# An encoder layer's expert stage: TensorE's loop over experts begins at block 4, with another order of the weight ring's homes

## Chip, cores, metric

One core of a Trainium2 chip runs the whole kernel. The metric is the device time of one execution in microseconds (us); lower is better.

## What is computed

The layer has three parts, in float32: a mixer with its projections, a cross attention, and a hierarchical mixture of experts with a final RMS norm. The change touches only the third part, which is this, for 256 tokens of width 2048 and 32 experts of which each token takes two:

```python
p_group = softmax(x @ w_rg)                       # 4 groups, one is taken
fine    = (x @ w_re)[that group]                  # 8 experts in it, the two best
gate    = p_group_best * softmax(top2)
for e in range(32):                               # each token goes to two of these
    y[tok] += gate * ((silu(x[tok] @ w1[e]) * (x[tok] @ w3[e])) @ w2[e])
h = h + y
out = rms_norm(h, norm_final)
```

`w1` and `w3` are 2048 x 512 per expert and `w2` is 512 x 2048: 4,096 KB each, 12,288 KB per expert, all of which are read whatever the tokens chose.

## The kernel before

**Blocks.** The expert stage is a row of blocks, one per expert, with 32 places for tokens; an expert with more tokens than that gets overflow blocks at the end, whose table `over_blocks` (VectorE, L2663) and `over_table` (L2689) work out, with one small product on TensorE between them (L1295). TensorE's part of block `n` is `block_n` (L1288): first the rest of the block before (`products`: `sums` at L1231, `rank_rows` at L1199, four `down` steps with W2 at L1247), then `gather` of the next block's tokens (L1187), then four `up` steps with W1 and four with W3 (L1219). Between the W3 steps stand the four `comb` steps of the block before (L1267), each of which waits for VectorE's `add` (L2588) of the step ahead. `down` of a block waits for VectorE's `gating` (L2570, semaphore `e_h`), `comb` for `picked` and `down_lo`. VectorE's program is written in the same order: gating, pick, `down_lo`, tokens, four adds, then the next block.

**The weight ring.** SyncE issues every load, in the order W1(0), W3(0), W2(0), W1(1), W3(1), W2(1), ... The q-th of these 4,096 KB matrices is called load q here, so that q = 3n - 1 is W2(n-1), 3n is W1(n) and 3n + 1 is W3(n). There are five homes of 32 KB per partition, numbered 0 to 4; `double_slots` (L173) says which home each load goes to. Before load q SyncE waits until TensorE has used the load that lay in that home last, and everything behind it in SyncE's program waits too. A load is one DMA of 4,096 KB (L632), save that home 1 is in two places and takes two of 2,048 KB (L573), and that the first and last loads are split (L573, L578, L626, L627).

Before, loads 0 to 16 go round the homes 0 1 2 3 4. From load 17 = 3 x 6 - 1 on, six loads make a turn over homes 2 3 4 0 1 4, so that in two blocks the ring returns to its start: W3 always lies in home 4 and waits for the W3 three loads back; all others wait for the load six back. The last loads, from 89, take the home that was used longest ago.

**Loops.** TensorE's program is written out for blocks 0 to 5; blocks 6 to 29 are a hardware loop of 12 passes of two blocks, and blocks 30 and 31 are written out again. ScalarE has the same start (`LOOP_AT`), VectorE's loop starts at block 7 whatever `LOOP_AT` is.

**Norm weights.** The 2048 weights of the final norm (`fgain`) are spread over all partitions by TensorE, 16 x 64 columns at a time, with 32 products of a 32 x 64 tile per half (L1284 and the weight loads that go with it), into PSUM banks 6 and 7; ScalarE copies the 1024 columns of each half out (L1791). One half goes ahead of block 3, the other ahead of block 4; each waits until the adds of the block before have ended, because `comb` uses the same banks. The small product of the overflow table stands ahead of block 5 (`OV_AT`), and `over_blocks` stands behind block 2's part in VectorE's program.

Of the kernel before, what the change touches and what calls it, by code (L numbers as in the profile page):

```python
# [16 lines left out]
ACT = mybir.ActivationFunctionType  # L17
# [7 lines left out]
P = 128  # L25
# [10 lines left out]
NE = 32  # L36
NG = 4
PG = NE // NG
ECH = 4
# [5 lines left out]
OVG = 8  # L45
ROWS = D // GW
NO_ROW = 2 * T * ROWS * ROWS
OV_AT = 5
LOOP_AT, LOOP_N = 6, 24
GAIN_AT = (3, 4)  # L50
GAIN_ROWS = 32
assert OVB % OVG == 0
EPS = 1e-6
# [119 lines left out]
def double_slots(order):  # L173

    first, last = 3 * LOOP_AT - 1, 3 * (LOOP_AT + LOOP_N) - 1
    homes = [q % 5 for q in range(first)]
    turn = [(first + r) % 5 for r in range(5)]
    turn.append(turn[2])
    homes += [turn[r % 6] for r in range(last - first)]
    while len(homes) < len(order) // 2:  # L180
        homes.append(min(range(5), key=lambda d: max(q for q, at in enumerate(homes) if at == d)))
    return homes


# [50 lines left out]
def flat(v):  # L235
    if len(v.shape) == 3:
        return v.rearrange("p a b -> p (a b)")
    return v.rearrange("p a b c -> p (a b c)")
# [12 lines left out]
def program(nc, ins, out, dbg=None):  # L251
    dbg = dbg or {}
    with ExitStack() as ctx:
# [16 lines left out]
        gate_sel, ident = front[:, 108 + KT:124 + KT], front[:, 124 + KT:124 + KT + P]  # L270
# [4 lines left out]
        ps = ctx.enter_context(nc.psum_tensor("ps", [P, 8, 512], F32))  # L275
# [84 lines left out]
        fgain, sq_out = arena(56, D), extra(0, 1024)  # L360
        gain_cut = D // GAIN_ROWS
# [44 lines left out]
        order = load_order()  # L406
# [52 lines left out]
        S = {}  # L459
# [200 lines left out]
        @block.gpsimd  # L660
        def _(pool):
            nc.gpsimd.memset(one_pp, 1.0).then_inc(S["pool_step"], 1)
            nc.gpsimd.memset(gone, 1.0).then_inc(S["pool_step"], 1)
            nc.gpsimd.memset(buf["mv"][:, :, :, P:P + 1], 1.0).then_inc(S["pool_step"], 1)
            for s in range(2 * HG_LEVELS):
                w, half = s // HG_LEVELS, 1 << (s % HG_LEVELS)
                u = 0 if w == 0 else 1
                cut = lambda x: flat(x).rearrange("p (b u t) -> p b u t", u=2, t=half)[:, :, u, :]
                pool.wait_ge(S["h_exp"], s + 1)
                if s >= 1:  # L670
                    pool.wait_ge(S["h_pe"], s)
                nc.gpsimd.tensor_tensor(cut(hqk[s % 2]), cut(he[s % 2]), cut(buf["hff" if w == 0 else "hfb"]),
                                        ALU.mult).then_inc(S["h_mulk"], 1)


            def gained(m):

                for q in (0, 2):
                    j = DONE[q][1]
                    pool.wait_ge(S["c_add"], m * 4 + (q + 1))  # L680
                    nc.gpsimd.tensor_tensor(hg[:, j, 0:1024], h[:, j, 0:1024], fgain[:, 0:1024], ALU.mult).then_inc(S["f_gain"], 1)

            pool.wait_ge(S["gain_act"], len(GAIN_AT))
            pool.wait_ge(S["tab_dve"], 1)
            nov = pool.value_load(table[0:1, 96:97], min_val=0, max_val=OVB)
            pool.wait_ge(S["up_used1"], (NE - 1) * ECH)
            nc.gpsimd.tensor_copy(z_fold, bc_mid(stack, P // EB)).then_inc(S["z_pool"], 1)
            for b in range(ROWS):
                own = slice(EB * b, EB * (b + 1))
                pool.wait_ge(S["z_pool"], 1 + b)  # L690
                nc.gpsimd.tensor_copy(z_gain[own, :], fgain[own, GW * b:GW * (b + 1)]).then_inc(S["z_pool"], 1)
            pool.wait_ge(*z_is("gain"))
            gained(NE - 2)
            pool.wait_ge(S["out_done"], 16 * NT)
            pool.wait_ge(*z_is("out"))
            nc.gpsimd.indirect_dma_start(out[0].rearrange("t (b n) -> (t b) n", n=GW), bass.IndirectOffsetOnAxis(z_row, 0), z_out, None,
                                         bounds_check=T * ROWS - 1, oob_is_err=False).then_inc(S["rows_done"], 16)
            with pool.Fori(0, OVB // OVG) as a:
                with pool.If(a * OVG < nov):
                    with pool.Fori(0, OVG) as c:  # L700
                        gained(a * OVG + c + NE - 1)
# [5 lines left out]
        def _(pe):  # L707
# [543 lines left out]
            def comb(of, q, b0=6, behind=0, at=None):  # L1251

                n = of.done
                u, j = (q // 2, q % 2) if at is None else at
                if q == 0:
                    pe.wait_ge(S["pick_all"], n + 1)
                    pe.wait_ge(S["ev_lo"], n + 1)
                if of.turn is None and of.like + 1 in GAIN_AT and q == 0:
                    pe.wait_ge(S["gain_act"], GAIN_AT.index(of.like + 1) + 1)
                if of.turn is None and of.like == OV_AT - 1 and q == 0:  # L1260
                    pe.wait_ge(S["tab_dve"], 1)
                if not (isinstance(n, int) and 4 * n + q <= behind):
                    pe.wait_ge(S["c_add"], n * 4 + (q - behind))
                for part in (d_hi, d_lo):
                    for b in range(2):
                        rows_ = slice(EB * (2 * u + b), EB * (2 * u + b + 1))
                        last = mm(ps[:, b0 + b, :], pick[rows_, j * P:(j + 1) * P], part[rows_, :],  # L1267
                                  start=(part is d_hi), stop=(part is d_lo))
                last.then_inc(S["c_pe"], 1)
# [5 lines left out]
                for i in range(ECH):  # L1275
                    down(at, i)

            def spread_gain(part, back):

                pe.wait_ge(S["fgain_in"], 16)  # L1280
                pe.wait_ge(S["c_add"], 4 * back.n)
                for r in range(GAIN_ROWS // 2):
                    k, c0 = part * GAIN_ROWS // 2 + r, r * gain_cut
                    last = mm(ps[:, 6 + c0 // 512, c0 % 512:c0 % 512 + gain_cut], ident[0:GAIN_ROWS, k:k + 1].to_broadcast([GAIN_ROWS, P]), gain_rows,  # L1284
                              start=True, stop=True)
                last.then_inc(S["gain_pe"], 1)

            def block_n(at, back, par, then=True, counts=False):  # L1288

                if at.like in GAIN_AT and at.turn is None:  # L1290
                    spread_gain(GAIN_AT.index(at.like), back)
                if counts:
                    pe.wait_ge(S["r_dve"], 4)
                    pe.wait_ge(S["c_add"], 4 * back.n)
                    mm(ps[:, 7, 0:2 * OVB], ones, flat(ov_rhs), start=True, stop=True).then_inc(S["r_pe"], 1)  # L1295
                if back is not None:
                    products(back)
                    if then:
                        gather(at.n + 1)
                for i in range(ECH):  # L1300
                    up(at, 0, i, par)
                if back is None and then:
                    gather(at.n + 1)
                for i in range(ECH):
                    up(at, 1, i, par)
                    if back is not None:
                        comb(back, i)
# [39 lines left out]
            block_n(Block(0), None, 0)  # L1347
            for n in range(1, LOOP_AT):
                block_n(Block(n), Block(n - 1), n % 2, counts=(n == OV_AT))
            with pe.Fori(0, LOOP_N // 2) as a:  # L1350
                n = a * 2 + LOOP_AT
                before_n, even, odd = Block(n - 1, LOOP_AT - 1, a), Block(n, LOOP_AT, a), Block(n + 1, LOOP_AT + 1, a)
                block_n(even, before_n, 0)
                block_n(odd, even, 1)
# [20 lines left out]
        def _(act):  # L1375
# [412 lines left out]
            def spread_gain(part):  # L1788

                act.wait_ge(S["gain_pe"], part + 1)  # L1790
                fn(fgain[:, 1024 * part:1024 * (part + 1)], flat(ps[:, 6:8, :]), ACT.Copy).then_inc(S["gain_act"], 1)  # L1791

            def block_n(n, back):
                if isinstance(n, int) and n in GAIN_AT:
                    spread_gain(GAIN_AT.index(n))
                if back is not None:
                    silu(back)
                if back is not None:
                    down_out(back, back)
                up_out(n, 0)  # L1800
                up_out(n, 1)
# [64 lines left out]
            first_block(0)  # L1866
            for n in range(1, LOOP_AT):
                block_n(n, n - 1)
            with act.Fori(LOOP_AT, NE - 1) as e:
                block_n(e, e - 1)  # L1870
            act.wait_ge(S["tab_dve"], 1)
# [16 lines left out]
        def _(dve):  # L1888
# [819 lines left out]
            for j in range(NT):  # L2708
                last = V.tensor_copy(z_what[:, j, 0:1], weight[:, NE - 1, j:j + 1])
            last.then_inc(S["z_dve"], 1)  # L2710
            dve.wait_ge(S["gain_act"], len(GAIN_AT))
            nov = dve.value_load(table[0:1, 96:97], min_val=0, max_val=OVB)
            finish_n(NE - 2, NE - 2, NE - 2, 0, 0)
            rows_of_last()
# [39 lines left out]
```

## Time and profile before

| | us |
|---|---|
| median of 3 runs | 1781.37 |
| lowest, highest | 1779.4, 1783.01 |
| the profiled execution | 1779.85 |
| its span | 1777.8 |
| TensorE matmuls busy | 1559.8 (88%) |
| VectorE, ScalarE, GpSimd busy | 814.6, 506.4, 45.5 |
| moved by DMA | 559.82 MB, mean 315 GB/s |

The profile is of one execution. The span runs from its first instruction to its last; 2.05 us of the execution's time lie around it. The expert stage begins near 871 us and takes the rest. Granted clock is the share of TensorE's full clock (2.4 GHz) that it was given: 1.0 or 0.5 at any moment, something between in a mean.

### The profile page before, as it was taken

What the parts mean: (1) busy time and instruction counts of PE and PEld (TensorE: products, weight loads), DVE (VectorE), ACT (ScalarE), POOL (GpSimd) and SP (SyncE); (2) the same over time, 40 slices, a digit from 0 to 9 for tenths busy, and PEclk for the clock granted to TensorE, in tenths of its full rate; (3) what the DMA queues carried; (4) which work ended last, traced back from release to release, by engine and by line L of the source; (5) the groups of instructions that cost most, each with busy time, mean ns of one, the idle gap of its engine ahead of it and who ended that gap; (6) DMA issues with size and microseconds to landing.
All of it is one profiled execution on the core that took longest, in us unless ns stands there. A gap on an engine that the chain in (4) does not pass through costs nothing.

```text
span 1777.8 us, 24664 instructions
## 1 busy us (share of the span) xinstructions
PE 1559.8 (88%) x10444; PEld 965.0 (54%) x10444; DVE 814.6 (46%) x1171; ACT 506.4 (28%) x729; POOL 45.5 (3%) x31
## 2 busy tenths in 40 slices
PE   9999999999999999999899768787687777687776
PEld 8888888788877898888544222222122222122222
DVE  5666566799666554354434322223232323232223
ACT  6464354644455354343410000000000000000003
POOL 0000000033000000000000000000000000000001
PEclk9999999999999999999988877787877788877788
DMA  9755555454455556565799999999999999999998
GB/s 359 256 187 198 166 163 169 157 163 144 160 172 189 201 181 225 199 272 201 305 433 426 434 428 433 427 435 432 429 429 432 435 426 434 432 432 431 431 428 345
DMA packets 125418, 559.82 MB, mean 315 GB/s; under 512 B 8828, under 2 KB 66428, under 8 KB 107296
## 3 DMA queue, kind: packets, MB, share of 16 engines
q1 hardware_dynamic: 124112, 556.52, 78.7%
q10 hardware_dynamic: 1152, 2.10, 0.4%
q8 instruction: 55, 0.90, 0.2%
q14 instruction: 19, 0.16, 0.0%
q0 software_dynamic: 80, 0.15, 0.0%
HBM read 556.50 MB, written 2.36 MB: 314 GB/s over the span
## 4 chain that ended last, share of the span: by engine, by line
PE 63%; DMA 31%; DVE 4%; issue 1%; ACT 0%; SPq 0%; POOL 0%; DVEq 0%; ACTq 0%; POOLq 0%
DMA arena<-in_moe_w_dram 31%; PE ps L774 11%; PE ps L1219 9%; PE ps L809 6%; PE ps L811 6%; PE ps L810 6%; PE ps L775 6%; PE ps L1267 5%; DVE arena L2588 2%; PE ps L1247 1%; PE ps L803 1%; PE ps L804 1%; PE ps L805 1%; PE ps L1063 1%; PE ps L1044 1%; PE ps L1284 1%
## 5 line engine op out<-in xcount | busy, mean ns | idle before, releaser
L1219 PE MATMUL ps<-arena 128*32 128x512 f32 x1808 | 290.0, 752 | 168.0 <-DMA arena<-in_moe_w_dram 166.5
L1948 DVE TENSOR_TENSOR w_lo<-arena,w_hi 128x1024 fp32r<-128x1024 f32 x264 | 316.5, 1240 | 205.2 <-ACT w_hi L1436 204.2
L2588 DVE SCALAR_TENSOR_TENSOR arena<-ps,arena 128x1024 f32<-128x1024 f32 x124 | 159.2, 1284 | 427.9 <-PE ps L1267 427.9
L1436 ACT ACTIVATE w_hi<-arena 128x1024 fp32r<-128x1024 f32 x262 | 262.7, 1052 | 263.7 <-PE ps L811 125.7
L1219 PEld LDWEIGHTS ps<-arena 128*32 128x32 f32 x1808 | 51.1, 121 | 311.5 <-DMA arena<-in_moe_w_dram 167.4
L1774 ACT ACTIVATE arena<-ps 128x512 f32<-128x512 f32 x64 | 38.2, 597 | 580.8 <-PE ps L1219 580.8
L774 PE MATMUL ps<-x_both,w_hi 128*128 128x512 f32 x420 | 148.6, 398 | 0.0
L1247 PE MATMUL ps<-arena 128*32 128x512 f32 x992 | 132.3, 679 | 6.7 <-DMA arena<-in_moe_w_dram 6.1
L1267 PEld LDWEIGHTS ps<-d_hi,pick 32*128 32x128 f32 x248 | 28.9, 230 | 182.3 <-DVE arena L2588 136.5
L775 PE MATMUL ps<-x_both,w_lo 128*128 128x256 f32 x420 | 118.0, 281 | 0.0
L1267 PE MATMUL ps<-d_hi,pick 32*128 32x512 f32 x248 | 79.1, 635 | 19.7 <-DVE arena L2588 19.3
L774 PEld LDWEIGHTS ps<-x_both,w_hi 128*128 128x128 f32 x420 | 78.9, 188 | 19.3 <-issue 1.4
L774 PE MATMUL ps<-m_both,w_hi 128*128 128x512 f32 x240 | 86.4, 403 | 0.0
L2582 DVE TENSOR_TENSOR d_lo<-ps,d_hi 128x512 fp32r<-128x512 f32 x31 | 21.5, 692 | 135.5 <-ACT d_hi L1786 135.5
L775 PEld LDWEIGHTS ps<-x_both,w_lo 128*128 128x128 f32 x420 | 79.5, 189 | 0.3
L1247 PEld LDWEIGHTS ps<-arena 128*32 128x32 f32 x992 | 32.6, 124 | 85.0 <-issue 75.6
L775 PE MATMUL ps<-m_both,w_lo 128*128 128x256 f32 x240 | 67.4, 281 | 0.0
L1786 ACT ACTIVATE d_hi<-ps 128x512 fp32r<-128x512 f32 x31 | 18.5, 597 | 169.9 <-PE ps L1247 169.9
L809 PE MATMUL ps<-w_hi,x_both 128*128 128x512 f32 x160 | 63.3, 396 | 0.0
L774 PE MATMUL ps<-q_both,w_hi 128*128 128x512 f32 x180 | 63.3, 396 | 0.0
L1267 PE MATMUL ps<-d_lo,pick 32*128 32x512 f32 x248 | 62.5, 502 | 0.0
L811 PE MATMUL ps<-w_hi,x_both 128*128 128x512 f32 x160 | 62.4, 390 | 0.0
(403 smaller groups left out, 2425.8 us busy)
## 6 DMA issues: line engine op xcount, KB each, us to landing
arena<-in_moe_w_dram SPq DMA_DIRECT2D x68, 4096.0 KB, 28.5
arena<-in_moe_w_dram SPq DMA_DIRECT2D x32, 2048.0 KB, 36.3
arena<-in_w_in_dram SPq DMA_DIRECT2D x51, 1024.0 KB, 5.0
extra<-in_moe_w_dram SPq DMA_DIRECT2D x17, 2048.0 KB, 32.5
arena<-in_xa_wk_dram SPq DMA_DIRECT2D x16, 1024.0 KB, 5.2
arena<-in_xa_wv_dram SPq DMA_DIRECT2D x16, 1024.0 KB, 5.0
arena<-in_w_out_dram SPq DMA_DIRECT2D x16, 1024.0 KB, 5.1
arena<-in_xa_wq_dram SPq DMA_DIRECT2D x16, 1024.0 KB, 5.3
```

Of the source, the lines that this page charges most:

```text
L774: mm(*whole_, start=(k == 0), stop=False, skip_group_check=True)
L775: last = mm(*part_, start=False, stop=False, skip_group_check=True)
L809: mm(o_, a_hi[:, k, rows_], hi, start=(k == 0), stop=False)
L810: mm(o_, a_hi[:, k, rows_], lo, start=False, stop=False)
L811: last = mm(o_, a_lo[:, k, rows_], hi, start=False, stop=(k == KT - 1))
L1219: last = mm(ps[EB * c:EB * (c + 1), m, :], xe[par][:, ECH * i + c, :], piece(at.like, m, i)[:, c, :], start=(i == 0), stop=(i == ECH - 1))
L1247: last = mm(ps[EB * b:EB * (b + 1), 4, :], hT[:, i, :], piece(at.like, 2, i)[:, b * 512:(b + 1) * 512], start=(i == 0), stop=(i == ECH - 1))
L1267: last = mm(ps[:, b0 + b, :], pick[rows_, j * P:(j + 1) * P], part[rows_, :], start=(part is d_hi), stop=(part is d_lo))
L1436: fn(hi_ring[(2 * n + u) % 4][:], ring_a[i][:, 2 * u:2 * u + 2, :], ACT.Copy).then_inc(S["w_hi"], 1)
L1774: fn(up_ev[:, m, :].rearrange("p (c q) -> p c q", c=ECH), ps[:, m, :].rearrange("p (q c) -> p c q", c=ECH), ACT.Copy).then_inc(S["ev_g" if ...
L1948: V.tensor_tensor(w_lo[i][:, 2 * u:2 * u + 2, :], ring_a[i][:, 2 * u:2 * u + 2, :], hi_ring[(2 * n + u) % 4][:].bitcast(F32), ALU.subtract ...
L2588: V.scalar_tensor_tensor(hv, flat(ps[:, b0:b0 + 2, :]), weight_of(e, j), hv, ALU.mult, ALU.add).then_inc(S["c_add"], 1)
```

## The change

TensorE's and ScalarE's loops begin at block 4, not 6 (13 passes of two blocks on TensorE). With that the six-load turn begins at load 3 x 4 - 1 = 11 and goes over homes 1 2 3 4 0 3; home 3 now has the short wait of three loads. The last seven loads get their homes by a written list. The overflow table is made two blocks sooner: `over_blocks` behind block 0's part on VectorE, `over_table` behind block 1's, the small product ahead of block 3. Both halves of the norm weights are spread between block 3 and the loop, the second into banks 2 and 3, and TensorE waits there for both of ScalarE's copies. GpSimd's copies for the last rows wait for W2 of block 30 instead of W3, because their place is now freed by it.

```diff
-OV_AT = 5
-LOOP_AT, LOOP_N = 6, 24
-GAIN_AT = (3, 4)
+OV_AT = 3
+LOOP_AT, LOOP_N = 4, 26
+GAIN_PARTS = 2
...
-    while len(homes) < len(order) // 2:
-        homes.append(min(range(5), key=lambda d: max(q for q, at in enumerate(homes) if at == d)))
+    homes += [turn[r] for r in (0, 1, 3, 4, 2, 3, 1)]
+    assert len(homes) == len(order) // 2
...
-            pool.wait_ge(S["up_used1"], (NE - 1) * ECH)
+            pool.wait_ge(S["dn_used"], (NE - 1) * ECH)
...
-                if of.turn is None and of.like + 1 in GAIN_AT and q == 0:
-                    pe.wait_ge(S["gain_act"], GAIN_AT.index(of.like + 1) + 1)
...
-            def spread_gain(part, back):
+            def spread_gain(back):
 
                 pe.wait_ge(S["fgain_in"], 16)
-                pe.wait_ge(S["c_add"], 4 * back.n)
-                for r in range(GAIN_ROWS // 2):
...
+                pe.wait_ge(S["e_h"], back)
+                pe.wait_ge(S["c_add"], 4 * back)
+                for part in range(GAIN_PARTS):
+                    for r in range(GAIN_ROWS // 2):
+                        k, c0 = part * GAIN_ROWS // 2 + r, r * gain_cut
+                        b0 = 6 - 4 * part + c0 // 512
+                        last = mm(ps[:, b0, c0 % 512:c0 % 512 + gain_cut], ident[0:GAIN_ROWS, k:k + 1].to_broadcast([GAIN_ROWS, P]), gain_rows,
+                                  start=True, stop=True)
+                    last.then_inc(S["gain_pe"], 1)
+                pe.wait_ge(S["gain_act"], GAIN_PARTS)
...
-                if at.like in GAIN_AT and at.turn is None:
-                    spread_gain(GAIN_AT.index(at.like), back)
...
             for n in range(1, LOOP_AT):
                 block_n(Block(n), Block(n - 1), n % 2, counts=(n == OV_AT))
+            spread_gain(LOOP_AT - 1)
             with pe.Fori(0, LOOP_N // 2) as a:
...
-                if isinstance(n, int) and n in GAIN_AT:
-                    spread_gain(GAIN_AT.index(n))
...
             for n in range(1, LOOP_AT):
                 block_n(n, n - 1)
+            for part in range(GAIN_PARTS):
+                spread_gain(part)
             with act.Fori(LOOP_AT, NE - 1) as e:
                 block_n(e, e - 1)
```

Loads 12 to 21, where the two orders first differ (home, and the load that must be used first):

| load | before | after |
|---|---|---|
| 12 to 15: W1(4), W3(4), W2(4), W1(5) | homes 2 3 4 0, five loads back | the same |
| 16: W3(5) | home 1, after load 11, W2(3) | home 3, after load 13, W3(4) |
| 17: W2(5) | home 2, after 12, W1(4) | home 1, after 11, W2(3) |
| 18: W1(6) | home 3, after 13, W3(4) | home 2, after 12, W1(4) |
| 19: W3(6) | home 4, after 14, W2(4) | home 3, after 16, W3(5) |
| 20, 21: W2(6), W1(7) | homes 0 1, after 15, 16 | homes 4 0, after 14, 15 |
| 94: W3(31) | home 2, after 89, W2(29) | home 4, after 91, W3(30) |

## Rows read from the trace of the kernel before

**Rows 1.** The page, the span in 40 slices of 44.4 us
```profile
GB/s 359 256 187 198 166 163 169 157 163 144 160 172 189 201 181 225 199 272 201 305 433 426 434 428 433 427 435 432 429 429 432 435 426 434 432 432 431 431 428 345
```
**Rows 2.** Busy time by stretch: engines, granted clock, DMA share, GB/s
```profile
875.00:880.00 5.00, 5.00 (x48) 1.53 (x52) 1.24 (x9) 0.60 (x1) 0.00 (x0) 1.00 0.62 221
...
880.00:1768.00 888.00, 689.57 (x5266) 231.11 (x5258) 263.80 (x391) 79.99 (x148) 7.48 (x7) 0.80 1.00 430
...
1006.00:1012.00 6.00, 5.60 (x28) 1.36 (x32) 0.00 (x0) 0.00 (x0) 0.00 (x0) 0.50 1.01 437
```
**Rows 3.** TensorE's waits for weights from 850 us on: total us, times, longest
```profile
PE ps L1219 <- DMA arena<-in_moe_w_dram: 166.5, 41, 7.8
```
**Rows 4.** SyncE's issues by time (start, us taken): loads 15 and 18
```profile
948.48 0.33 SPq L632 DMA_DIRECT2D arena<-in_moe_w_dram  x1
...
978.37 0.33 SPq L632 DMA_DIRECT2D arena<-in_moe_w_dram  x1
```
**Rows 5.** Issue to landing, us, issues at 876.92, 908.33, 948.48, 1035.54, 1707.85
```profile
arena<-in_moe_w_dram SPq DMA_DIRECT2D x1, 1024.0 KB, 5.9
...
arena<-in_moe_w_dram SPq DMA_DIRECT2D x1, 4096.0 KB, 29.9
...
arena<-in_moe_w_dram SPq DMA_DIRECT2D x1, 4096.0 KB, 38.4
...
arena<-in_moe_w_dram SPq DMA_DIRECT2D x1, 4096.0 KB, 20.1
...
arena<-in_moe_w_dram SPq DMA_DIRECT2D x1, 2048.0 KB, 39.5
```
**Rows 6.** The page's issues, of loads with an empty queue ahead of them
```profile
arena<-in_xa_wv_dram SPq DMA_DIRECT2D x16, 1024.0 KB, 5.0
```
**Rows 7.** VectorE by time: block 1's gating; first and last of over_blocks (30 operations)
```profile
904.25 0.28 DVE L2570 TENSOR_TENSOR arena<-ps,arena 128x128 f32<-128x128 f32 x1
...
950.78 0.17 DVE L2666 TENSOR_SCALAR arena<-arena 128x32 f32<-128x32 f32 x1
...
956.87 0.37 DVE L2686 TENSOR_SCALAR arena<-front,arena 128x16 f32<-128x16 f32 x2
```
**Rows 8.** TensorE by time: W2 steps of block 1 and of block 5
```profile
904.63 3.64 PE L1247 MATMUL ps<-arena 128*32 128x512 f32 x32
...
1006.40 6.61 PE L1247 MATMUL ps<-arena 128*32 128x512 f32 x32 [3.60 <-DMA arena<-in_moe_w_dram]
```
**Rows 9.** TensorE by time: from the end of block 2 to that of block 5
```profile
920.89 0.39 PE L1267 MATMUL ps<-d_lo,pick 32*128 32x512 f32 x2
922.76 6.23 PE L1284 MATMUL ps<-diag,front 32*128 32x64 f32 x32 [1.48 <-DVE arena L2588]
...
951.01 7.06 PE L1284 MATMUL ps<-diag,front 32*128 32x64 f32 x32 [1.48 <-DVE arena L2588]
957.99 1.92 PE L1231 MATMUL ps<-arena 128*64 128x32 f32 x32
...
980.91 0.38 PE L1295 MATMUL ps<-arena 128*128 128x32 f32 x2 [1.48 <-DVE arena L2588]
981.22 1.55 PE L1231 MATMUL ps<-arena 128*64 128x32 f32 x32
...
1000.71 0.39 PE L1267 MATMUL ps<-d_lo,pick 32*128 32x512 f32 x2
```
**Rows 10.** ScalarE by time: the copy of the second half of the norm weights
```profile
958.10 1.02 ACT L1791 ACTIVATE arena<-ps 128x1024 f32<-128x1024 f32 x1 [9.02 <-PE ps L1284]
```
**Rows 11.** TensorE by time: the first products behind the loop's first return
```profile
1065.29 1.12 PE L1231 MATMUL ps<-arena 128*64 128x32 f32 x32
```
**Rows 12.** The tail: TensorE's last step with W3(30); GpSimd's copies
```profile
1735.50 1.06 PE L1219 MATMUL ps<-arena 128*32 128x512 f32 x8
...
1737.01 2.61 POOL L691 COPY arena<-arena 32x512 f32<-32x512 f32 x4
1747.15 2.39 POOL L681 TENSOR_TENSOR arena<-arena 128x1024 f32<-128x1024 f32 x1 [7.53 <-DVE arena L2588]
```

More of the change, by code:

```diff
@@ L681, in gained @@
                     nc.gpsimd.tensor_tensor(hg[:, j, 0:1024], h[:, j, 0:1024], fgain[:, 0:1024], ALU.mult).then_inc(S["f_gain"], 1)
-            pool.wait_ge(S["gain_act"], len(GAIN_AT))
+            pool.wait_ge(S["gain_act"], GAIN_PARTS)
             pool.wait_ge(S["tab_dve"], 1)
             nov = pool.value_load(table[0:1, 96:97], min_val=0, max_val=OVB)
-            pool.wait_ge(S["up_used1"], (NE - 1) * ECH)
+            pool.wait_ge(S["dn_used"], (NE - 1) * ECH)
             nc.gpsimd.tensor_copy(z_fold, bc_mid(stack, P // EB)).then_inc(S["z_pool"], 1)
@@ L1276, in products @@
                     down(at, i)
-            def spread_gain(part, back):
+            def spread_gain(back):
                 pe.wait_ge(S["fgain_in"], 16)
-                pe.wait_ge(S["c_add"], 4 * back.n)
-                for r in range(GAIN_ROWS // 2):
[L1283 to L1286, printed above, removed]
+                pe.wait_ge(S["e_h"], back)
[8 more added lines that the diff above has]
+                pe.wait_ge(S["gain_act"], GAIN_PARTS)
             def block_n(at, back, par, then=True, counts=False):
-                if at.like in GAIN_AT and at.turn is None:
-                    spread_gain(GAIN_AT.index(at.like), back)
                 if counts:
@@ L1790, in spread_gain @@
                 act.wait_ge(S["gain_pe"], part + 1)
-                fn(fgain[:, 1024 * part:1024 * (part + 1)], flat(ps[:, 6:8, :]), ACT.Copy).then_inc(S["gain_act"], 1)
+                b0 = 6 - 4 * part
+                fn(fgain[:, 1024 * part:1024 * (part + 1)], flat(ps[:, b0:b0 + 2, :]), ACT.Copy).then_inc(S["gain_act"], 1)
             def block_n(n, back):
-                if isinstance(n, int) and n in GAIN_AT:
-                    spread_gain(GAIN_AT.index(n))
                 if back is not None:
@@ L2710, in _ @@
             last.then_inc(S["z_dve"], 1)
-            dve.wait_ge(S["gain_act"], len(GAIN_AT))
+            dve.wait_ge(S["gain_act"], GAIN_PARTS)
             nov = dve.value_load(table[0:1, 96:97], min_val=0, max_val=OVB)
```

## The prediction

> **What bounds the kernel now.** I read the page's slices first. From the slice that begins near 890 us on, the core moves 426 to 435 GB/s until the end [rows 1]. The stretches say the same more sharply: from 880 to 1768 us the DMA engines are busy the whole time (share 1.00) and move 430 GB/s, while TensorE is busy 690 of 888 us [rows 2]. The waits follow from that: TensorE stood 166.5 us for weights [rows 3]. So from 880 us on the end is set by one stream of 4,096 KB loads, each of which takes 4.19 MB / 430 GB/s = 9.75 us. A change in this stage can cost time only where it leaves the stream without a load, and can win time only by filling a hole or raising the rate. There is no hole to fill behind 885 us; the one ahead (875 to 880 us, share 0.62 [rows 2]) comes from block 0's first steps, which the change doesn't touch.
>
> The thing to read is therefore not how late TensorE is, but how much is queued in front of a load when SyncE issues it. The issue-to-landing times tell it. A load with nothing ahead needs its 9.75 us and a fixed part: a 1,024 KB load in the dense part lands 5.0 us after its issue [rows 6], of which its data take 2.4, so 2.6 us are fixed, and a 4,096 KB load would need 12.4 us. Load 10, issued at 908.33, landed 29.9 us later [rows 5], so 17.5 us were queued ahead of it. Load 15, issued at 948.48 [rows 4], took 38.4 [rows 5] and landed at 986.9. The load at 1035.54, the first of the steady state, took 20.1, so 7.8 us lay ahead.
>
> **The change, part by part.** All numbers are in the times of the profiled execution (1779.85 us, with a span of 1777.8; the median of the runs is 1781.37, 1.5 us more, so the sum is added to that).
>
> 1. *The ring.* In the steady state nothing differs: before and after, W3 waits for the W3 three loads back, and the five others of a turn for six loads back. The homes are renamed. Where the turn begins it differs: load 16, W3(5), waited for load 11, W2(3), and now waits for load 13, W3(4). In the time of before that moves its issue to 978.37, when load 18 was issued on the same event [rows 4]. Even so load 16 would come before load 15 lands at 986.9. Taken alone, the new order costs nothing: the cover is 986.9 - 2.6 = 984.3 us, the last moment at which load 16 can be issued with the stream unbroken. The margin is 984.3 - 978.4 = 5.9 us. The rest of the sum asks what else delays W3(4)'s last step.
>
> 2. *over_blocks behind block 0.* The 30 small VectorE operations run from 950.78 to 956.87 + 0.37, that is 6.46 us [rows 7]. They hid behind the first half of the norm weights' pause then. Now they stand ahead of block 1's gating, which began at 904.25 [rows 7], 0.4 us ahead of the W2 steps that need it, at 904.63 [rows 8]. Queued behind the gating on VectorE are pick, d_lo, tokens and the adds; TensorE's W2 steps of block 1 start at 904.63 + 6.5 = 911.1. There is no cover.
>
> 3. *The clock behind that pause.* TensorE then idles 6.4 us. Where it idled 3.6 us ahead of the W2 steps of block 5, these took 6.61 us against 3.64 for those of block 1 [rows 8]; the granted clock was 0.50 from 1006 to 1012 us [rows 2]. I take the same here: +3.0 us. Between nothing and 3.0 I choose 3.0, since the row's pause was the shorter one. Blocks 1 and 2 are then 9.5 us late. The loads issued in this stretch have 17.5 us ahead of them [rows 5], so the stream doesn't notice.
>
> 4. *Block 3 starts without the norm weights and with the small product.* Block 2's last comb ended at 920.89 + 0.39 = 921.3 [rows 9], now 930.8. At block 5 the wait for the last add (1.48) and the small product (981.22 - 980.91) put 1.8 us between the last comb and the sums [rows 9]. So the sums of block 3 start at 932.6. From there I take block 5, which had its product and all its weights: from 981.22 to its last comb at 1000.71 + 0.39, 19.9 us [rows 9]. Block 3 ends at 952.5.
>
> 5. *The norm weights, both halves.* First the wait for the last add, 1.5 us [rows 9]. Then 64 products. The first 32 took 6.23 us, the second 7.06 [rows 9], and and I take the slower pace for both, 2 x 7.06 = 14.1. Then TensorE waits for the copy of the second half, which began 0.03 us behind the last product and takes 1.02 [rows 10], with 0.15 us to wake: 1.2 us. Before, this copy ran beside the sums. The sums of block 4 start at 952.5 + 1.5 + 14.1 + 1.2 = 969.3; before, at 957.99 [rows 9]. The 14.1 us of products themselves aren't new (they were 6.23 + 7.06); they now lie all ahead of block 4, the first half of them no longer ahead of block 3.
>
> 6. *Load 16.* From block 4's sums to its last W3 step it took 978.37 - 957.99 = 20.4 us [rows 4, 9]. Its weights have landed (load 13 was ahead of 15 in the same stream). So W3(4) is used at 989.7, and load 16 is issued 989.7 - 984.3 = 5.4 us too late. The stream stands still that long and nothing gives it back. Load 16 lands at about 1002 and loads 17 and 18 go out with it, so load 19 has nearly two loads ahead.
>
> By the Trainium skill, DMA: Bandwidth & Descriptors, section "Anatomy of one DMA", the fixed part is about 2.0 us, most of it the receipt after the last byte; an estimate by that page makes the stall 4.8 us, not 5.4. The rows of this trace say 2.6.
>
> 7. *Loops and tail.* At the loop's first return no idle time stands ahead of the sums of block 8 [rows 11], so passes are free. Load 94 now waits for W3(30), whose last step ended at 1735.50 + 1.06 = 1736.6 [rows 12]; load 93's second half, issued at 1707.85, landed 39.5 us later, at 1747.3 [rows 5]. The margin is 1747.3 - 2.6 - 1736.6 = 8.1 us: nothing. GpSimd's copies (2.61 us and a 0.29 us one) begin some 6.5 us later, at the end of block 30's W2 steps near 1743.3, and end at 1746.2, under the 1747.15 where its next operation waited for an add anyway [rows 12]. Nothing; without that cover it would be a us or two on GpSimd, beside the stream's last loads.
>
> Sum: +5.4 us, thus 1785.3 for the profiled execution and 1781.4 + 5.4 = 1786.8 for the median.
>
> **Ends of the unknown costs.** No loss of clock behind the first pause: -3.0. Norm weights at the first half's pace twice: -1.6. Both together put load 16 at 985.1, which still costs 0.8 us. The other way: block 4 stays at the lower clock for all its W2 steps and gather, up to +3.0 (the 3.0 of part 3 once more), and the restart costs what it did at 876.92, where a 1,024 KB load took 5.9 us and not 5.0 [rows 5, 6], +0.9: 9.3 us. So 0.8 to 9.3.
>
> **Rivals.**
> *A, the stream isn't broken enough to see.* TensorE is quicker than I sum up, W3(4) is used before about 987.9 and the loss is below 3.6 us: 1781.4 to 1785. For it: the margin was 5.9 us, and two of the additions (clock, pace of the products) come from stretches with another history. Against it: block 4's sums start 969.3 - 957.99 = 11.3 us later by the sum, and without the clock's 3.0 they are still 8.3 late, more than the margin.
> *B, the early loop starves again and again.* If the late start didn't heal in block 5, or if the loop's returns cost TensorE time, the next W3 loads would miss too: three such misses of 3 to 5 us give 1781.4 + 5.4 + 10 = 1797. It decides if load 19 is issued more than 17 us behind the landing of load 16; I expect 17 - 7.8 = 9, as in the steady state, where the load at 1035.54 had 7.8 us queued ahead [rows 5]. By the Trainium skill, Runtime: NRT & Kernel Launch, section "Instruction fetch mechanics", a taken branch out of the fetched pages stalls the sequencer, which speaks against more blocks in loops; the trace shows no such idle time at the return.
> *C, faster.* The stream runs at a better rate, because home 1, with its two DMAs of 2,048 KB, now holds W2 of odd blocks, where it held W1. To be seen the rate must rise from 430 by 0.4% over 888 us, 3.6 us; with the stall of 5.4 in place it would need 1%: 1776 without the stall. For it only that the slices scatter from 426 to 435 [rows 1]. Against it: both matrices are read in the same pieces, and one DMA fewer is split of some 130.
> *D, nothing happens at all*: the early pauses vanish in the queue and the homes don't matter: 1781.4, the edge of A.
>
> **Chances.** 0.2% of 1781.37 is 3.6 us, about what a measurement can tell from no change. The forecast (a loss of 3.6 to 9.3 us) 0.67, A with D 0.22, B 0.05, C 0.06. Slower by over 0.2%: 0.67 + 0.05 = 0.72; within: 0.22; faster: 0.06. The likeliest time is 1786.8. The range takes A's upper two thirds and the forecast to its end and leaves out B, C and the rest of A: 1781.8 to 1790.5.
>
> **What would show it.** The 30 operations near 904 to 911 us, and TensorE's W2 steps of block 1 behind them, slow. About 14 us of the 64 products from about 954 us. Load 16's issue near 990 us, the DMA share well under 1.00 between 985 and 995 us, and a landing 12 to 13 us after its issue. After that 430 GB/s again, and a tail as before, all about 5 us later. I'd be wrong if load 16's issue-to-landing time is above 15 us (a load still ahead), or if the share stays at 1.00 there and the time has changed all the same.

## The result

The changed kernel takes 1786.56 us (median of 9 runs, 1783.31 to 1792.55), the kernel before 1781.53 in its 9. The ratio is 1.003 with a 95% interval of 1.0019 to 1.004: it is 3.4 to 7.1 us slower. The forecast was 1786.8.

The stretches of the changed kernel, with the columns of [rows 2] (length, the engines' busy time, granted clock, DMA share, GB/s):

```profile
980.00:985.00 5.00, 4.62 (x42) 1.27 (x36) 1.28 (x1) 0.60 (x1) 0.00 (x0) 1.00 0.88 372
985.00:990.00 5.00, 4.22 (x40) 1.30 (x40) 2.81 (x3) 0.60 (x1) 0.00 (x0) 1.00 0.33 105
990.00:995.00 5.00, 5.00 (x68) 2.38 (x68) 1.93 (x5) 0.28 (x1) 0.00 (x0) 1.00 0.84 354
995.00:1000.00 5.00, 5.00 (x48) 1.30 (x40) 2.10 (x3) 0.60 (x1) 0.00 (x0) 1.00 1.01 433
1000.00:1770.00 770.00, 599.21 (x4388) 188.17 (x4384) 221.01 (x305) 67.18 (x126) 7.47 (x7) 0.79 1.00 431
```

This is the whole loss. In the 20 us from 980 on, the stream moves 5 x (372 + 105 + 354 + 433) = 6320 units of us x GB/s where 430 GB/s would give 8600: it lacks 2280 / 430 = 5.3 us. From 1000 us to the end it moves 431 GB/s, with no second hole. The profiled execution (1783.31) is the fastest of the nine and 3.46 us above that of before (1.4 us of which lie ahead of the expert stage), so it shows the place better than the size.

SyncE's issues of loads 15 and 16, by time, answer to [rows 4]:

```profile
951.32 0.33 SPq L632 DMA_DIRECT2D arena<-in_moe_w_dram  x1
...
988.66 0.33 SPq L632 DMA_DIRECT2D arena<-in_moe_w_dram  x1
```

and their times from issue to landing (last column, us) to [rows 5]:

```profile
arena<-in_moe_w_dram SPq DMA_DIRECT2D x1, 4096.0 KB, 35.9
...
arena<-in_moe_w_dram SPq DMA_DIRECT2D x1, 4096.0 KB, 13.1
```

Load 15 lands at 951.32 + 35.9 = 987.2, and load 16 goes out only then, at 988.66, 0.07 us behind the last step with W3(4) (TensorE by time, 987.53 + 1.06 = 988.59):

```profile
987.53 1.06 PE L1219 MATMUL ps<-arena 128*32 128x512 f32 x8
```

It lands 13.1 us later, near the 12.4 us of a load with nothing ahead of it, at 1001.8. Two landings in an unbroken stream are 9.75 us apart; these are 14.5 apart, so 4.8 us are missing. This distance, landing to landing less 9.75, is called the gap in what follows.

VectorE and TensorE up to that issue, by time:

```profile
905.65 0.17 DVE L2668 TENSOR_SCALAR arena<-arena 128x32 f32<-128x32 f32 x1
...
911.73 0.37 DVE L2688 TENSOR_SCALAR arena<-front,arena 128x16 f32<-128x16 f32 x2
```
```profile
912.35 5.36 PE L1247 MATMUL ps<-arena 128*32 128x512 f32 x32 [6.25 <-DVE arena L2572]
...
932.50 1.59 PE L1231 MATMUL ps<-arena 128*64 128x32 f32 x32
...
951.98 0.40 PE L1265 MATMUL ps<-d_lo,pick 32*128 32x512 f32 x2
953.85 13.88 PE L1285 MATMUL ps<-diag,front 32*128 32x64 f32 x64 [1.47 <-DVE arena L2590]
969.29 1.92 PE L1231 MATMUL ps<-arena 128*64 128x32 f32 x32 [1.56 <-ACT arena L1793]
```

The 30 operations stand between block 0's adds and block 1's gating, TensorE idles 6.25 us behind them, and its W2 steps then take 5.36 us against 3.64 in [rows 8]. The 64 products take 13.88 us, the wait for ScalarE's copy 1.56. Block 4's sums start at 969.29; the sum had said 969.3. That they agree so closely is chance: the stage began 1.4 us later in this execution than in that of before (SyncE's first issue of it at 878.32 instead of 876.92 us), so 9.9 us of lateness are the change's, where 11.3 were forecast.

### The profile page after: what moved, and what is told of

The parts are those of the page before. It is cut to its first block, busy times and chain, and to the rows that moved or that the text cites. A ratio compares the mean times of both kernels' runs of the same rounds, so it can differ in the third digit from the quotient of the medians.

```text
span 1781.3 us, 24710 instructions
## 1 busy us (share of the span) xinstructions
PE 1574.0 (88%) x10444; PEld 967.1 (54%) x10444; DVE 815.4 (46%) x1171; ACT 506.8 (28%) x729; POOL 44.4 (2%) x31
## 4 chain that ended last, share of the span: by engine, by line
PE 63%; DMA 30%; DVE 5%; issue 1%; ACT 1%; SPq 0%; POOL 0%; DVEq 0%; ACTq 0%; POOLq 0%
DMA arena<-in_moe_w_dram 30%; PE ps L774 11%; PE ps L1219 9%; PE ps L809 6%; PE ps L811 6%; PE ps L810 6%; PE ps L775 6%; PE ps L1265 5%; DVE arena L2590 2%; PE ps L1247 1%; PE ps L1285 1%; PE ps L1063 1%; PE ps L1044 1%; PE ps L803 1%; PE ps L804 1%; PE ps L805 1%
```

## The experiments

Theory 1 is the prediction's: a gap in the stream ahead of load 16, which needs both a late TensorE and the new wait for W3(4). Theory 2: the early loop and the renamed ring cost the time by themselves. Theory 3: a late TensorE is enough. All kernels are edits of the changed kernel. Ratios are to the kernel before, whose median was 1781.4 and 1781.5 us in the same two sessions. A ratio need not be the quotient of the two medians; they differ by up to 0.0006.

**Old ring.** `LOOP_AT, LOOP_N = 6, 24`, the homes and GpSimd's wait as before, and:

```diff
                 block_n(Block(n), Block(n - 1), n % 2, counts=(n == OV_AT))
-            spread_gain(LOOP_AT - 1)
+                if n == 3:
+                    spread_gain(3)
```

> The changed kernel with the ring and the loops of before (loop from block 6, load 16 waits for W2(3) in home 1), but with its late TensorE: over_blocks behind block 0, both halves of the norm weights behind block 3. Theory 1 (the loss is one hole ahead of load 16, from a late TensorE and the new wait for W3(4) together): no hole, load 16 issued near 976 us, DMA share 1.00 throughout, 1781.5 us, as before. Theory 2 (the early loop and the new ring cost the time somewhere, whatever the lateness): 1781.5 too. Theory 3 (a late TensorE is enough, the ring doesn't matter): 1786.5 us, as changed.

1781.77 us, ratio 1.0004 (0.9994 to 1.0014). TensorE is as late as in the changed kernel (64 products behind block 3, block 4's sums at 971.33 us, in an execution whose stage began 2.0 us later), and it costs nothing that can be measured: load 16 follows load 15 by 9.8 us from landing to landing. Theory 3 falls.

**Table behind block 3.**

```diff
-                if n == OV_AT - 3:
+                if n == 2:
                     over_blocks()
-                if n == OV_AT - 2:
                     over_table()
...
             spread_gain(LOOP_AT - 1)
+            pe.wait_ge(S["r_dve"], 4)
+            mm(ps[:, 7, 0:2 * OVB], ones, flat(ov_rhs), start=True, stop=True).then_inc(S["r_pe"], 1)
+            pe.wait_ge(S["tab_dve"], 1)
```

> The changed kernel, ring and loops as changed, but over_blocks, the small product and over_table all between block 3 and the loop, beside the 64 products. Theory 1: TensorE comes to load 16's wait about 8 us sooner (6.5 and what the clock cost, less about 1 us for the small product there), near 980 us, with the stream still running: no hole, 1781.5 us. Theory 2: 1786.5 us. Theory 3: 1781.5 to 1782.

1782.69 us, ratio 1.0001 (0.9989 to 1.0012), so the time of before comes back within what can be measured. That speaks against theory 2, since ring and loops are the changed ones. But the trace says that the expectation's road there was wrong. TensorE by time in this run:

```profile
939.83 1.94 PE L1219 MATMUL ps<-arena 128*32 128x512 f32 x8 [5.75 <-DMA arena<-in_moe_w_dram]
...
950.73 13.88 PE L1283 MATMUL ps<-diag,front 32*128 32x64 f32 x64 [1.48 <-DVE arena L2591]
965.72 0.64 PE L1350 MATMUL ps<-arena 128*128 128x32 f32 x2 [1.11 <-ACT arena L1794]
967.05 1.92 PE L1231 MATMUL ps<-arena 128*64 128x32 f32 x32 [0.69 <-DVE arena L2698]
```

Without the early pause TensorE is ahead of its weights in block 3 and stands 5.75 us for W3(3). In the changed kernel, with its early pause, TensorE doesn't wait for W3(3) at all: the pause had hidden this wait. Load 16 goes out at 987.74 us, not near 980, and a gap of 2.9 us is left (load 15 lands at 948.20 + 40.2 = 988.4, load 16 at 987.74 + 13.3 = 1001.0).

**More products.** In `spread_gain`, the second half twice:

```diff
-                    for r in range(GAIN_ROWS // 2):
+                    for r in list(range(GAIN_ROWS // 2)) * (1 + part):
```

> The changed kernel with the second half's 32 products done twice (96 instead of 64). Theory 1: the hole grows by all of their 7 us, to about 11: 1793.5 us. Theory 2: TensorE's pause hides under the stream, 1786.5. Theory 3: 1793.5.

1793.03 us, ratio 1.0067 (1.0054 to 1.0081). TensorE by time, W2 steps in block 3, then the products:

```profile
936.63 5.61 PE L1247 MATMUL ps<-arena 128*32 128x512 f32 x32
...
956.73 19.80 PE L1285 MATMUL ps<-diag,front 32*128 32x64 f32 x96 [1.48 <-DVE arena L2590]
```

The 96 products take 5.9 us more than 64, and load 16 lands at 998.54 + 13.4 = 1011.9, after load 15 at 988.7: the gap is 13.5 us, 8.7 more than in the changed kernel and 2.5 more than expected. Most of what the products don't explain is the clock: in this execution the W2 steps in blocks 3 and 4 took 5.61 and 3.64 + 2.23 us, in the changed kernel's 4.19 and 2.69 + 1.89. The time grew by 6.6 us, so lateness that the cover doesn't hide goes into the time nearly in full.

**Kept busy**, first try. In `products`, behind `rank_rows`, for block 1 (the bank is written over by the W2 steps that follow):

```diff
+                if at.turn is None and at.like == 1:
+                    pe.wait_ge(S["ev_d"], 1)
+                    pe.wait_ge(S["ev_lo"], 1)
+                    for _ in range(13):
+                        for b in range(4):
+                            mm(ps[EB * b:EB * (b + 1), 4, :], ident[:, 0:EB], hn[:, 0, 512 * b:512 * (b + 1)], start=True, stop=True)
```

> The changed kernel with 52 products of 128x512, whose results nobody reads, in TensorE's pause beside over_blocks. Theory 1: the clock stays at full rate, block 1's W2 steps take 3.6 us and not 5.4, load 16 is issued 1.7 us sooner and the hole is 1.7 us shorter: 1785 us. If the clock had no part in it: the same 5.4 us and 1786.5. Theory 2: 1786.5.

1786.91 us, ratio 1.0037 (1.0024 to 1.005): a miss of mine. The 52 products took 11.37 us, longer than the pause, so the W2 steps came later, though they did take 3.62 us. The gap is 7.1 us.

**Halves apart.** As the table behind block 3, and:

```diff
+                if n == 3:
+                    spread_gain(2, 0)
                 block_n(Block(n), Block(n - 1), n % 2)
-            spread_gain(LOOP_AT - 1)
+            spread_gain(3, 1)
+            pe.wait_ge(S["gain_act"], GAIN_PARTS)
```

> Ring and loops as changed; everything else where the kernel before had it: the first half of the norm weights ahead of block 3, the second behind it, over_blocks beside the second half, the small product between it and the loop. In the run with only the table moved, TensorE stood 5.75 us for W3(3) in block 3 and came to load 16's wait hardly sooner. Theory 1, so amended (the pauses ahead of block 4 minus what they hide of that wait): the first 32 products now lie in the place of the 5.75 us, load 16 is issued near 981 us, 5 us before load 15 has landed less the fixed part, no hole: 1781.5 us. Theory 2 (ring and early loop cost time by themselves): 1785 or more.

ScalarE copies the first half ahead of block 3 too, and the first `comb` behind it waits for that copy. 1782.89 us, ratio 1.0006 (0.9995 to 1.0016). TensorE by time:

```profile
926.03 5.23 PE L1285 MATMUL ps<-diag,front 32*128 32x64 f32 x32 [1.48 <-DVE arena L2596]
...
954.32 6.13 PE L1285 MATMUL ps<-diag,front 32*128 32x64 f32 x32 [1.48 <-DVE arena L2596]
...
962.88 1.92 PE L1231 MATMUL ps<-arena 128*64 128x32 f32 x32 [0.69 <-DVE arena L2703]
```

The first products now fill the place where TensorE would stand for W3(3), block 3 waits for no weights, and load 16 goes out at 982.99 us, with load 15 still to land at 989.2. From issue to landing of load 16:

```profile
arena<-in_moe_w_dram SPq DMA_DIRECT2D x1, 4096.0 KB, 15.9
```

That is 3.5 us more than the 12.4 of an empty queue, and 2.3 more than the longest restart measured (13.6): the stream didn't break. The gap is 0. Ring and loops are the changed ones, so by themselves they cost nothing that can be measured (at most 2.9 us, the end of the interval): theory 2 falls.

**Halves apart, early pause back** (`over_blocks` behind block 0 again).

> As the run before it, but with over_blocks behind block 0, as changed: the norm weights' halves apart, the early pause back. Theory 1, amended: the wait for W3(3) is filled already by the early pause, so splitting the products hides none of them; load 16 near 988 us, a hole of about 4 us, 1786 us. If it were the two halves standing together that costs the time: no hole, 1781.5.

1786.89 us, ratio 1.003 (1.0018 to 1.0042), the time of the changed kernel. Load 16 goes out at 992.04 us and lands at 1005.3, load 15 landed at 989.0: a gap of 6.6 us, where about 4 were expected. So it isn't that the two halves stand together. The one wait of 5.75 us hides one pause ahead of it, the early one or the first products, and here both stand there.

**Kept busy, second try**: the same edit with `range(7)`, 28 products.

> The changed kernel with 28 products of 128x512 in TensorE's pause beside over_blocks, whose results nobody reads (52 took 11.4 us, longer than the pause). Theory 1: they end within the pause, block 1's W2 steps take 3.6 us and not 5.4, load 16 comes 1.7 us sooner, the hole is 3 us instead of 4.8: 1785 us. Without a part of the clock: 1786.5.

1784.55 us, ratio 1.0016 (1.0007 to 1.0025). TensorE by time:

```profile
906.30 6.21 PE L1278 MATMUL ps<-arena,front 128*32 128x512 f32 x56
912.64 3.64 PE L1247 MATMUL ps<-arena 128*32 128x512 f32 x32
```

The products end within the pause (the trace counts each as two), the W2 steps take 3.64 us instead of 5.36, and load 16 goes out at 987.57, when load 15 lands: a gap of 3.7 us, 1.1 less than in the changed kernel. The granted clock is 1.00 from 905 to 920 us; in the changed kernel it is 0.50 from 910 to 915. That work which nobody reads keeps the clock there, and makes the W2 steps 1.7 us shorter, is shown. That it makes the whole kernel faster is likely and not shown: the median is 2.0 us lower, and seven of the changed kernel's nine executions are slower than all ten of these, but the two were timed in different sessions and the intervals of their ratios overlap. Nor is the 1.1 us of gap clear of scatter: the next W2 steps, in block 3, took 5.34 us here and 4.19 in the changed kernel.

**Old ring, more products.** The old ring with 96 products.

> The changed kernel with the ring and loops of before, and the second half's 32 products done twice (96 products behind block 3). Theory 1: load 16 waits for W2(3), near 985 us, about when the stream can still take it, loads 17 and 18 follow in time: at most 1 us of hole, 1781.5 to 1783, where the same 7 us cost 6.5 us in the new ring. Theory 3 (lateness alone costs): 1788 or more.

1781.61 us, ratio 1.0002 (0.9993 to 1.001). This and the run with more products differ in ring, loops and GpSimd's wait alone. Issue to landing of load 16's two DMAs, at 983.79 and 985.51 us:

```profile
extra<-in_moe_w_dram SPq DMA_DIRECT2D x1, 2048.0 KB, 10.2
...
arena<-in_moe_w_dram SPq DMA_DIRECT2D x1, 2048.0 KB, 13.4
```

Both go out before load 15 lands at 989.1; the second lands at 998.9, a gap of 0. With the same 96 products the kernel loses 11.9 us in the new ring and nothing that can be measured in the old one, where load 16 waits for the first thing that block 4 does with weights (W2(3)), not for its last (W3(4)).

| kernel | load 16 issued | load 15 landed | gap, us | ratio - 1, x 1781.4 us |
|---|---|---|---|---|
| before | 964.7, 966.5 | 986.9 | 0 | 0 |
| old ring | 978.0, 980.3 | 989.4 | 0 | 0.7 (-1.1 to 2.5) |
| old ring, more products | 983.8, 985.5 | 989.1 | 0 | 0.4 (-1.2 to 1.8) |
| halves apart | 983.0 | 989.2 | 0 | 1.1 (-0.9 to 2.9) |
| table behind | 987.7 | 988.4 | 2.9 | 0.2 (-2.0 to 2.1) |
| kept busy, 28 products | 987.6 | 987.6 | 3.7 | 2.9 (1.2 to 4.5) |
| changed | 988.7 | 987.2 | 4.8 | 5.3 (3.4 to 7.1) |
| halves apart, early pause | 992.0 | 989.0 | 6.6 | 5.3 (3.2 to 7.5) |
| kept busy, 52 products | 991.7 | 988.4 | 7.1 | 6.6 (4.3 to 8.9) |
| more products | 998.5 | 988.7 | 13.5 | 11.9 (9.6 to 14.4) |

The gap, read from one profiled execution each, goes with the times of all ten kernels and lies within the interval of all but one; the 2.9 us of the table behind block 3 lie above its 2.1 (its median is 1.3 us above that of before). Four of the six times with a gap lie some 0.5 to 1.6 us under it, one 2.7 under and one 0.5 above. Little of that is won back in the stream: by the bytes of the traces' DMA packets, the same data, from about 1035 us to about 1755 us of the changed kernel, took 719.4 to 719.6 us in the six kernels with a gap and 719.9 to 720.2 in the four without, about half a microsecond.

No version beat the kernel before, and none could by this road: the best that any edit here can do is a gap of 0.

## Why the prediction was right

*The bound.* Right: the loss is a hole in the weight stream, and only about half a microsecond of it is given back.

*Step 1, the ring.* Right, and shown from both sides: the new ring with little lateness (halves apart) and the old ring with the whole of it cost nothing that can be measured; only both together do. The cover of 984.3 us was read rightly: with the landing of this execution it is 987.2 - 2.6 = 984.6, and the issue at 988.66 is 4.1 us behind it.

*Steps 2 and 3, the early pause and the clock.* The pause was 6.25 us (6.4 forecast). The clock made the W2 steps 1.7 us longer, not 3.0: the granted clock was 0.50 from 910 to 915 us and 0.91 from 915 to 920. It had fallen within the pause, ahead of the steps, and came back in the middle of them. That is the mis-sized term. The second run with busy products shows that it is real. Step 2 misreads one row: the 30 operations (950.78 to 957.24 us) ran beside the second half's products (951.01 to 958.07, [rows 9]), not the first half's. The sum doesn't hang on it. Step 2's "There is no cover" was true of the gating, but not of what the pause is worth. Taking it away wins only some 2 us of gap, not 9.5, mainly because TensorE then stands 5.75 us for W3(3). Step 4 took block 3's relief of 6.5 us as if nothing were late next; that holds only as long as the early pause is there.

*Steps 4 and 5.* 19.9 us forecast for block 3 from its sums to its last comb, 951.98 + 0.40 - 932.50 = 19.9 measured. Products 13.88 us (14.1), the wait for ScalarE's copy 1.56 (1.2).

*Step 6.* The issue was 988.66 us; with the 1.4 us by which this execution's stage began later, 989.7 would have been 991.1. Of the 2.4 us between, 1.3 are the clock of step 3, and 1.0 is block 4, which took 19.4 us from its sums to the issue instead of 20.4. The restart took 13.1 us from issue to landing, 0.7 above the 12.4 of the sum and inside its upper end of 0.9; in the six kernels with a gap it was 13.1 to 13.6, that is 3.4 to 3.9 us above the data's 9.75 and not 2.6.

The Trainium skill's fixed part of about 2.0 us (DMA: Bandwidth & Descriptors, "Anatomy of one DMA", a section on DMAs that GpSimd issues; these are SyncE's) would make it 11.8, as an estimate; the measurements don't agree, and they decide.

That the gap of 4.8 us comes so near to the 5.4 of the sum is in part luck. The issue was 2.4 us earlier than forecast, which alone leaves 3.0. But load 15 landed at 987.2, and with the later start it should have been 986.9 + 1.4 = 988.3: the cover ended 1.1 us sooner. And the restart took 0.7 us more. 3.0 + 1.1 + 0.7 = 4.8. The stated range doesn't quite follow from its own sum either: losses of 0.8 to 9.3 us would give 1782.2 to 1790.7, not 1781.8 to 1790.5.

*Step 7.* The loops' returns cost nothing that can be measured (halves apart: ratio 1.0006, at most 1.0016), and at the first of them in the changed kernel, ahead of block 6, the sums start at 1009.79 us with no idle time before them. The tail's new short wait shows, and is hidden. Issue of load 94's first half, and its issue to landing:

```profile
1735.75 0.33 SPq L573 DMA_DIRECT2D arena<-in_moe_w_dram  x1
```
```profile
arena<-in_moe_w_dram SPq DMA_DIRECT2D x1, 2048.0 KB, 20.1
```

For 2,048 KB, 4.9 us of data and 2.6 fixed, 12.6 us were queued ahead.

*Rivals.* A's times (1781.4 to 1785) are where five of the experiments ended, but not the changed kernel. B didn't occur: one gap, then 431 GB/s. Load 19, on which B hung, was issued at 1008.8 us, 7.0 behind the landing of load 16 (9 were expected), and landed 22.2 us later, so 9.8 us were queued ahead of it: one load, not the "nearly two" of step 6. C would have needed a better rate; it is 431 against 430, and it doesn't show in the kernels whose gap is 0.

## What to carry to other kernels

Where a stream of transfers sets the end, price an edit by the last moment at which each transfer can be issued with the stream unbroken (the landing of the one before it, less the fixed part; 2.6 us by the row used here, 3.4 to 3.9 by the restarts measured), not by busy time: in these ten kernels lateness up to there was free, and behind it nearly every microsecond counted. Two harmless edits can share one margin: here a buffer order that waits for the last use in a block instead of the first, and pauses moved to one side of it. And when a pause is taken away, ask what is late next before crediting it.

## What hadn't been expected of the hardware

Products that do nothing but keep TensorE busy for 6.21 us left the granted clock at full rate, and the steps behind them took 3.64 us instead of 5.36.

In one execution the time above the median was made in the last 50 us. The profiled execution of the halves apart took 1787.4 us, 4.5 above that kernel's median, though its stream never broke. Two stretches of its tail, and its last W2 steps (TensorE by time):

```profile
1735.00:1740.00 5.00, 5.00 (x22) 1.20 (x16) 2.29 (x2) 0.38 (x1) 0.00 (x0) 0.50 0.93 397
1740.00:1745.00 5.00, 5.00 (x48) 3.12 (x48) 2.18 (x5) 0.50 (x2) 0.00 (x0) 0.50 1.01 426
```
```profile
1769.70 6.02 PE L1247 MATMUL ps<-arena 128*32 128x512 f32 x32 [0.45 <-DVE arena L2578]
```

The clock is at half rate where the changed kernel had 0.99 and 1.00, and the last W2 steps wait for no weights: TensorE is the late one there. In the changed kernel's execution the last of these steps waited for its weights:

```profile
1770.63 1.06 PE L1247 MATMUL ps<-arena 128*32 128x512 f32 x8 [0.73 <-DMA arena<-in_moe_w_dram]
```

That the clock in the tail makes the scatter in general is read from these two executions and wasn't tested.
